# A two-block transformer on one core: the first mixer's input projection as three products of rounded parts, and half of the first layer's modulation blocks moved into the output projection

## What is computed

```python
mod = (silu_c @ ada_w[i] + ada_b[i])[:, None, :]          # 1024 x 6144, for x and for ctx
sh1, sc1, gt1, sh2, sc2, gt2 = jnp.split(mod, N_MOD, axis=-1)
h = modulate(rms_norm(x, norm_g[i, 0]), sh1, sc1)
hc = modulate(rms_norm(ctx, norm_g[i, 0]), sh1c, sc1c)
# even_mixer
u = h @ w_in                                              # w_in: 1024 x 2048
uc = hc @ w_in
y = jnp.concatenate([pool_mixer(u[..., :D_POOL], pool_w, pool_scale),
                     neighbourhood_attention(q, k, v, k_c, v_c, rpb)], axis=-1) @ w_out
x = x + gt1 * rms_norm(y, norm_g[i, 1])
h = modulate(rms_norm(x, norm_g[i, 2]), sh2, sc2)
```

## Time and profile before

| | |
|---|---|
| median of 3 runs | 2689.47 us (2688.32 to 2698.58) |
| the profiled execution | 2697.27 us, span 2695.4 us |
| mean granted TensorE clock | 0.93 |
| TensorE matmul busy | 2411.7 us (89%) |
| VectorE busy | 1732.8 us (64%) |
| ScalarE busy | 1002.2 us (37%) |
| GpSimd busy | 65.0 us (2%) |
| weight loads | 318 of 1 MB, 33.3% of the DMA engines' time |

### The profile page before, as it was taken

How to read it: one execution, slowest core, us unless ns; L and a number is a source line. 1 busy time by engine, 2 the same in 40 slices (tenths; PEclk the granted TensorE clock), 3 DMA queues, 4 the chain that set the end, 5 groups by cost and what they waited for, 6 DMA issues and landing times.

```text
span 2695.4 us, 46035 instructions
## 1 busy us (share of the span) xinstructions
PE 2411.7 (89%) x19796; PEld 1951.5 (72%) x19796; DVE 1732.8 (64%) x3316; ACT 1002.2 (37%) x1876; POOL 65.0 (2%) x70
## 2 busy tenths in 40 slices
PE   7699988999997996888888889988979999997998
PEld 6366437877875485787888689987667879667786
DVE  6875349776646267667666587865455765654577
ACT  1004333223222134344332254344344654553465
POOL 0300000000000000000000000011000001000000
PEclk9898699999998998999999899988779999997999
DMA  7351024666542100000001267841034853102475
GB/s 294 141 198 36 16 78 170 239 224 226 203 156 96 69 0 2 3 3 3 3 11 65 80 252 279 306 146 66 1 131 183 341 207 131 39 1 94 170 297 204
DMA packets 47275, 347.95 MB, mean 129 GB/s; under 512 B 5248, under 2 KB 5248, under 8 KB 5728
## 3 DMA queue, kind: packets, MB, share of 16 engines
q1 hardware_dynamic: 45936, 334.52, 33.3%
q0 software_dynamic: 1136, 10.50, 1.0%
HBM read 343.95 MB, written 1.05 MB: 128 GB/s over the span
## 4 chain that ended last, share of the span: by engine, by line
PE 72%; DVE 22%; ACT 4%; issue 2%; DMA 1%; DVEq 0%; ACTq 0%; POOLq 0%
PE banks L533 20%; PE banks L926 8%; PE banks L1786 4%; DVE arena L611 4%; PE banks L1021 3%; PE banks L2531 3%; PE banks L2532 3%; PE banks L2533 3%; PE banks L1000 3%; PE banks L1663 2%; PE banks L1857 2%; PE banks L786 2%; PE banks L1254 2%; PE banks L2562 1%; PE banks L2564 1%
## 5 line engine op out<-in xcount | busy, mean ns | idle before, releaser
L611 DVE SCALAR_TENSOR_TENSOR arena<-weight_slots,silu_c,arena 128x256 f32<-128x256 f32 x776 | 329.2, 499 | 0.0
L514 DVE TENSOR_TENSOR moe_w_low<-weight_slots,moe_w_high 128x2048 fp32r<-128x2048 f32 x96 | 218.1, 2290 | 71.8 <-ACT moe_w_high L505 70.9
L926 PE MATMUL banks<-arena,weight_slots 128*128 128x256 f32 (+1 forms) x768 | 230.8, 459 | 17.1 <-DVE arena L1578 11.7
L926 PEld LDWEIGHTS banks<-arena,weight_slots 128*128 128x128 f32 x768 | 149.2, 195 | 94.9 <-issue 75.3
L514 DVE TENSOR_TENSOR mlp_w_low<-weight_slots,mlp_w_high 128x2048 fp32r<-128x2048 f32 x64 | 146.4, 2288 | 106.7 <-ACT mlp_w_high L505 106.6
L505 ACT ACTIVATE moe_w_high<-weight_slots 128x2048 fp32r<-128x2048 f32 x96 | 181.3, 1911 | 26.0 <-PE banks L2564 19.7
L1786 PE MATMUL banks<-weight_slots,arena 64*64 64x64 f32 (+1 forms) x3648 | 151.9, 226 | 37.1 <-DVE weight_slots L2099 15.5
L505 ACT ACTIVATE mlp_w_high<-weight_slots 128x2048 fp32r<-128x2048 f32 x64 | 122.2, 1909 | 158.2 <-PE banks L533 140.9
L1786 PEld LDWEIGHTS banks<-weight_slots,arena 64*64 64x64 f32 x3648 | 142.7, 137 | 45.1 <-issue 16.1
L2531 PE MATMUL banks<-moe_w_high,slots_x 128*128 128x512 f32 x320 | 133.5, 417 | 11.8 <-DVE moe_w_low L514 11.8
L1938 ACT ACTIVATE weight_slots<-banks 128x512 f32<-128x512 f32 x80 | 47.8, 597 | 233.2 <-DVE weight_slots L2099 204.8
(11 more groups left out here) (371 smaller groups left out, 5137.2 us busy)
## 6 DMA issues: line engine op xcount, KB each, us to landing
weight_slots<-weights SPq DMA_DIRECT2D x318, 1024.0 KB, 4.8
arena<-small POOLq DMA_DIRECT2D x1, 2560.0 KB, 9.1
arena<-x_t POOLq DMA_DIRECT2D x1, 2048.0 KB, 16.7
arena<-bias POOLq DMA_DIRECT2D x1, 2048.0 KB, 9.5
constants<-consts POOLq DMA_DIRECT2D x1, 1395.0 KB, 21.3
out_t<-arena SPq DMA_DIRECT2D x1, 1024.0 KB, 3.9
parameters<-params POOLq DMA_DIRECT2D x1, 775.0 KB, 10.0
arena<-pool_inv POOLq DMA_DIRECT2D x1, 512.0 KB, 10.4
```

The costliest lines, as they stand in the source:

```text
L514: nc.vector.tensor_tensor(self.pair(j)[1], slot(j, 0, SLOT), self.pair(j)[0], ALU.subtract).then_inc(*v.step("used", j))
L611: nc.vector.scalar_tensor_tensor(a_, w, c, a_, ALU.mult, ALU.add).then_inc(*v.step())
L926: ins = nc.tensor.matmul(psum(b, 0, w), slot(j, k, 256, i * P, P), moving(k), start=(k == 0), stop=(k == KT - 1))
```

## The change

The block order of the first layer becomes 8 modulation blocks, two projection blocks, then six projection blocks mixed with eight modulation blocks, and then the four blocks of the output projection mixed with the other eight modulation blocks. The input projection rounds activations and weights and makes three products of them, on TensorE in the lines of `Splits`; the weights have two pairs of buffers. ScalarE rounds and evicts every tile; VectorE makes the remainders and its chains. The rounded high parts of the activations lie where the squares of the norm were, the low parts over the activations themselves. The accumulators of the chains are a ring of two in the input projection and of four after it. The pooling waits for the fourth tile alone. The vectors of the last four modulation chunks are made after the output projection, and TensorE's sums for them stand at its end.

```diff
-    order = ["mod0"] * FIRST_MODS + mixed(("ev_in", 8), ("mod0", 24 - FIRST_MODS)) + ["ev_out"] * 4
+    order = ["mod0"] * FIRST_MODS + ["ev_in"] * 2 + mixed(("ev_in", 6), ("mod0", 8)) + mixed(("ev_out", 4), ("mod0", 8))
...
-            if j >= FIRST_MODS and v.chains >= 4:
-                v.wait_ge(*after("mod_summed", *v.chained[v.chains - 4]))
+            slots = 2 if v.chains < 8 else 4
+            if j >= FIRST_MODS and v.chains >= slots:
+                v.wait_ge(*after("mod_summed", *v.chained[v.chains - slots]))
...
-        chain_sums.update({mod_of(j): MACC[:, i % 4] for i, j in enumerate(rest)})
+        IN_ACC, OUT_ACC = area(38848, 2, 2, 256), area(37424, 4, 2, 256)
+        chain_sums.update({mod_of(j): IN_ACC[:, i % 2] for i, j in enumerate(rest[:8])})
+        chain_sums.update({mod_of(j): OUT_ACC[:, i % 4] for i, j in enumerate(rest[8:16])})
+        chain_sums.update({mod_of(j): MACC[:, i % 4] for i, j in enumerate(rest[16:])})
...
-            g.wait_ge(*after("taken_all", "ev_in"))
-            g.wait_ge(*after("taken_all2", "ev_in"))
+            g.wait_ge(*after("taken", "ev_in", 3))
...
+        EV_IN = Splits("ev_in", ["ev_in"], [(30656, 32704), (34752, 36800)])
+
         def ev_in_tensor(pe):
+            pe.stage("project_ev_in")
+            for n in range(6):
+                j = EV_IN.next(pe, "ev_in")
+                for i in range(2):
+                    b = take_bank(pe, ("ev_in", 2 * n + i))
+                    ins = EV_IN.columns(pe, j, 256, i * P, psum(b), KT, lambda k: IN_HI[:, :, k, :],
+                                        lambda k: XLO2[:, :, k, :], norm="n1_0")
+                    ins.then_inc(*pe.step("ev_in", 2 * n + i))
+                pe.mark("multiplied", j)
+            for n in range(2):
+                j = EV_IN.next(pe, "ev_in")
+                for seg in range(2):
+                    b = take_bank(pe, ("ev_v", n, seg))
                     for half_ in range(2):
+                        t = slice(half_ * P, (half_ + 1) * P)
+                        for m, (x, part) in enumerate([(IN_HI, 0), (IN_HI, 1), (XLO2, 0)]):
+                            for k in range(KT):
+                                ins = nc.tensor.matmul(psum(b, half_ * 256, 256), x[:, seg, k, t],
+                                                       EV_IN.pair(j)[part][:, k * 256:(k + 1) * 256],
+                                                       start=(m == 0 and k == 0), stop=(m == 2 and k == KT - 1))
+                    ins.then_inc(*pe.step("ev_v", n, seg))
+                pe.mark("multiplied", j)
...
+        def ev_in_scalar(act):
+
+            act.stage("project_ev_in")
+            act.wait_ge(*after("pads"))
+            for n in range(8):
+                EV_IN.high(act, n + EV_IN.ahead)
+                if n < 6:
+                    for g in (2 * n, 2 * n + 1):
+                        act.wait_ge(*after("ev_in", g))
+                        nc.scalar.activation(ev_place(g), psum(bank_of(("ev_in", g))).rearrange("p (s t) -> p s t", t=SEQ),
+                                             ACT.Copy).then_inc(*act.step("taken", "ev_in", g))
...
+        def ev_in_vector(v):
+
+            v.stage("project_ev_in")
+            for n in range(8):
+                EV_IN.low(v, n + EV_IN.ahead)
...
                            banks=range(6), then=y_sums(pe, "x01", BOTH))
+            side_blocks(pe, block_of["mlp1_0"][0], 0)
             x_sums_tensor(pe, "n2_0", [X, CTX])
...
-            modulate_scalar(act, "n1_0", 0, 0, BOTH)
-            ev_out_of(act, 0, act_copy)
+            EV_IN.high(act, 0)
+            high_scalar(act, "n1_0", 0, 0, BOTH, BOTH[::-1])
+            ev_in_scalar(act)
...
-            ev_out_of(v, 1, dve_copy)
-            mod_vectors(v, 0, range(2, 6))
+            EV_IN.low(v, 0)
+            low_vector(v, "n1_0", 0, 0, BOTH, BOTH[::-1])
+            ev_in_vector(v)
             att_vector(v, LAT)
             att_vector(v, CON)
             v.stage("norm")
             MLP0.low(v, 0)
             MLP0.low(v, 1)
+            mod_vectors(v, 0, range(2, 6))
+            v.stage("norm")
```

More of the change, by code:

```diff
@@ L754, in modulate_vector @@
             v.mark("scaled_all", key)
[L756 to L762, removed]
         SQ_HIGH = area(16896, 2, KT, SEQ)
@@ L861, in high_scalar @@
+        def high_scalar(act, key, m, half, todo, segs):
             act.wait_ge(*after("mod_ready", m, mod_part(m, half)))
-            place = split_places(segs)
+            place = split_places(key, segs)
             for k in range(KT):
[L864 to L867, removed]
+                for seg in todo:
+                    act.wait_ge(*after("scaled", key, k, seg))
+                    nc.scalar.activation(place(k, seg)[0], HT[:, seg, k, :], ACT.Identity,
+                                         bias=mod_col(m, 3 * half, k, seg)).then_inc(*act.step("h_rounded", key, k, seg))
+                if todo[-1] == segs[0]:
@@ L1236, in pool_scalar @@
             act.mark("pool_done")
+        EV_IN = Splits("ev_in", ["ev_in"], [(30656, 32704), (34752, 36800)])
         def ev_in_tensor(pe):
[L1239 to L1247, removed]
-                for i in range(2):
[L1249 to L1253, removed]
-                        ins = nc.tensor.matmul(psum(b, 0, w), slot(j, k, 256, i * P, P), moving(k),
-                                               start=(k == 0), stop=(k == KT - 1))
-                    ins.then_inc(*pe.step(key, g + i))
-                pe.mark("used", j)
@@ L1259, in values_natural @@
-        def values_natural(pe, name, key, blocks, n_tok, width, segs=(0, 1)):
-            for jj in range(blocks):
-                j = next_block(pe, name)
-                for seg in range(n_tok // 2):
-                    b = take_bank(pe, (key, jj, seg))
-                    for half_ in range(2):
-                        for k in range(KT):
-                            s = segs[seg]
-                            ins = nc.tensor.matmul(psum(b, half_ * 256, 256), HT[:, s, k, half_ * P:(half_ + 1) * P],
-                                                   slot(j, k, 256), start=(k == 0), stop=(k == KT - 1))
-                    ins.then_inc(*pe.step(key, jj, seg))
-                pe.mark("used", j)
@@ L1273, in take_values @@
-        def take_values(q, key, blocks, n_tok, place, shares, copy):
-            for jj in range(blocks):
-                for seg in range(n_tok // 2):
-                    if (jj * (n_tok // 2) + seg) % 2 != shares:
-                        continue
-                    q.wait_ge(*after(key, jj, seg))
-                    b = bank_of((key, jj, seg))
-                    copy(place(jj, seg), psum(b).rearrange("p (t c) -> p t c", c=256)).then_inc(*q.step("taken", key, jj, seg))
-            q.mark(key + "_out", shares)
+            pe.stage("project_ev_in")
@@ L3272, in _ @@
             scaled_vector(v, "n1_3", 3, 0, X)
-            low_vector(v, "n1_3", 3, 0, X, ONE)
+            low_vector(v, "n1_3", 3, 0, ONE, ONE)
             od_vector(v)
```

60 lines of the change are left out of this document (27 added, 33 removed).

## The result

The changed kernel takes 2656.14 us (median of 4, 2654.95 to 2657.37) against 2690.89 us (median of 4) of the kernel before, measured beside it: ratio 0.9872, 95% interval 0.9859 to 0.9884. That is 34.8 us or 1.3% less; 33.3 were forecast. Its profiled execution has a span of 2653.2 us.

The account below looks back on a forecast made before the run. VectorE's 16 chains and evictions were taken to bound the input projection first, TensorE's four-pass products later. Input projection -40.6, attention -0.4, output projection +7.7 sum to -33.3 us from the 2689.5 median: 2656.2 us, range 2636 to 2677.

Parts of the forecast that it names:

- E1's end: Input projection: the second of its eight blocks ends at 88.9 us, and its last eviction starts the pooling at 89.5.
- the long chain's end: Input projection: VectorE's modulation chain beside GpSimd's pooling, 16 instructions of 1.34 us each, 21 us, ends at 116.
- the pair's second chain: Input projection: the second of two modulation chains ahead of the fifth block ends on VectorE at 122.1 us.
- the fifth block: Input projection: TensorE waits 11.9 us for its remainder, pays 2.4 us of low clock, runs it 124.4 to 137.7.
- rival (a): Input projection: pooling costs TensorE nothing, as VectorE's chains are not in its way; 12 us more gain, 2644; chance 0.15.
- the low level: Input projection: TensorE's clock at 1.2 instead of 2.4 GHz after a long wait, costing 2.4 us each time.
- The long remainder: Input projection: VectorE's 2.3 us weight remainder beside the pooling loses at most one GpSimd operation, 1.3 us; slowed proportionally, 7.6 us.
- The price of the products: Input projection: a block of rounded parts takes 10.9 us instead of 13.98, a block of values 11.5 us.
- (b): Attention: its clock comes out higher; context part at the high level saves at most 20.7 us, 2636; chance 0.12.
- (c): Attention, first part: clock stays low, up to 30 us dearer; for half the turns 15 us, 2671; chance 0.12.
- (d): Input projection: the split does not overlap, TensorE waits and starts low at six blocks; 26 us, 2682; chance 0.08.
- (e): Attention into output projection: TensorE's clock stays low throughout, 46.7 us dearer, 2703; chance 0.03.

Follow-up runs that it names:

- The move alone: Kernel before, products kept in float32, with eight of 16 modulation blocks moved from the input projection into the output projection: 2658.4 us, ratio 0.9882.
- the late pooling: Changed kernel with GpSimd's pooling held until the last value tile is evicted (2646.8 us), or until the last block's remainder is made (2645.2 us).
- rounded parts alone: Rounded-part products in the input projection as in the changed kernel, but all 16 modulation blocks stay there, accumulators a ring of two: 2699.7 us, ratio 1.0022.

## Why the prediction was right

**The projection** was right to the microsecond, and by its own steps. TensorE's start was forecast for 65.6 and was 65.0; E1's end 88.9 and 89.4; the pooling 89.5 to 115.7 and 90.3 to 116.2; the long chain's end 116 and 116.5; the pair's second chain 122.1 and 122.5; the fifth block 124.4 to 137.7 and 124.85 to 137.6; the stage 175.2 and 175.2. The move alone and the late pooling show that the two main steps are the true ones: VectorE's chains were last before, and one chain beside the pooling costs TensorE 12 us afterwards. With the pooling away the stage ends at 164.4, where rival (a) put it at 163.4. Two small terms were off and nearly cancelled: the low level cost the first block 2.7 us and the fifth 1.9, where the prediction had 2.4 for each.

The long remainder beside the pooling, at 92.05, took 2.90 us instead of 2.28, and not the 7.6 of a slowing in proportion. That agrees with the page SBUF — State Buffer of the Trainium skill (section Who interferes with whom): a lock for a whole instruction, so at most one GpSimd operation is lost.

A scaling of 512 columns with one SBUF input took 1.32 us beside the pooling and 0.49 behind it. The same page and section of the Trainium skill say that such an instruction contends in a two-port mode only; the trace agrees as far as it goes, since it does not show the mode.

**The price of the products** was right (10.9 us per block); the estimate that the prediction made from the page FP8 and Floating Point Precision of the Trainium skill (section TensorE Precision Notes), 10.5 us by four passes to three, is 0.4 us too low per block here. For a block of values it is 1.1 us too low (11.6 measured, 11.5 forecast from the rows).

**What each half is worth** the prediction did not say, and its sentence that TensorE's four-pass products bind "later" invites the reading that shorter products alone would help. The runs say: the move gives 32.5 of 34.8 us, the rounded parts alone nothing (+0.2%), and together with the move 2 to 3 us, because TensorE's saving is handed on: 11.6 us lie between the end of the fourth block (113.25) and the start of the fifth, where two sums take 1.8 undisturbed; the fifth block's low clock costs 1.9 us (124.85 to 137.60 against 10.9); the start is 5.7 us later than that of the move alone (64.96 against 59.22), and the first block loses 2.7 us to the low level.

**The attention** was forecast unchanged but for 0.4 us. It took 97.9 us against 102.3 and 100.5. The chain of waits shows where, first one row of the kernel before that belongs behind the second of the earlier trace rows, then the changed kernel:

```profile
235.84 1.07 PE banks L1000 x2
```

```profile
181.47 2.00 PE banks L1001 x2
...
186.41 1.15 PE banks L1001 x2
...
191.82 1.07 PE banks L1001 x2
```

The last row of each is the same step of the same turn: 20.1 us after the attention's start before (in both profiles) and 16.6 us in the changed kernel. So 3.5 us come from the low clock level, which lasted for one turn instead of three; this is the mechanism that rivals (b) and (c) named, at a small size, and why it lasted shorter no run shows. The other 0.9 us against the first profile are the last product ahead of the output projection, 4.50 us there against 3.66, and 3.65 in the second profile of the kernel before (granted clock 0.81, 1.00 and 1.00), so they are not the change's. The context part's turns stayed at 2.81 us.

**The output projection** was forecast at +7.7 us and took 69.8 against 62.6, +7.2. The MLP's first block was rounded 51.5 us after the stage's start (forecast 52), the last chain ended at 54.6 (55), and TensorE waited for no load.

**How near the total is** owes something to luck. Against the second profile of the kernel before, whose execution (2689.1) is nearer its median than the first one's, the projection ends 39.5 us earlier (forecast 40.6), the attention is 2.6 us shorter (0.4) and the output projection 7.2 us longer (7.7); what follows is 0.8 us longer. The sum is 34.1 us. What the attention gave without being forecast made up for what the projection fell short.

**The rivals.** (d) and (e) did not happen: apart from the one wait the blocks follow each other without a gap, and the output projection ran at clock 1.00. The rest of the difference between the two first profiles, 4.5 us behind the start of the residual, is not the change's: the second profile of the kernel before does not have it.

## What to carry to other kernels

When two engines take turns in being last in a stage, price each half of a change alone against the other's schedule: shorter matmuls were worth nothing while VectorE was last, 3 us of the stage after it was relieved, and 13 us once its contention with GpSimd was gone. Moving side work to a stage whose engine idles paid ten times as much as the shorter products did at first, and two and a half times as much as they did in the end. And before placing work on GpSimd, look for the stretch in which a slower VectorE holds nobody up; here that one wait was worth 10.8 us of the stage.

## What the runs showed of the hardware

A VectorE chain of 14 accumulations took 18.8 to 19.1 us beside GpSimd's additions in every kernel that had them together, whether TensorE worked through it (the move alone) or waited (rounded parts alone), and 5.6 us otherwise. An operation of GpSimd beside a remainder of 2048 columns took 3.22 instead of 1.3 us, and the remainder 2.90 instead of 2.28. The stretch of the low clock level at the start of the attention came out as one, two or three turns in kernels whose attention begins with the same matmuls, and as the same number in both profiles where a kernel has two; nothing in these runs says which it will be. Behind the residual's start one and the same kernel took 2314.8 us in one execution and 2309.5 in another.
